# Base and levels of one-headed decay units issued and placed in three groups

## What is computed

```python
def chunked_vector_decay(q, k, v, log_f):        # o_t = S_t^T q_t, S_t = diag(exp(log_f_t)) S_{t-1} + k_t v_t^T
    def step(state, inp):
        qc, kc, vc, fc = inp
        cum = jnp.cumsum(fc, axis=-2)
        rel = jnp.where(causal, cum[..., :, None, :] - cum[..., None, :, :], -jnp.inf)
        scores = jnp.einsum('bhtd,bhsd,bhtsd->bhts', qc, kc, jnp.exp(rel))
        o = (jnp.einsum('bhts,bhsv->bhtv', scores, vc)
             + jnp.einsum('bhtd,bhdv->bhtv', qc * jnp.exp(cum), state))
        ...
```

## Time and profile before

| | |
|---|---|
| median of 3 executions | 3364.64 us |
| lowest, highest | 3363.71, 3365.63 us |
| the profiled execution | 3369.68 us |
| its span, first to last instruction | 3367.6 us |
| mean granted clock of TensorE, as a share of 2.4 GHz | 0.993 |

### The profile page before, as it was taken

One profiled execution on the slowest core, in us unless ns is written; L12 is line 12 of the kernel. 1 busy time (PEld: TensorE's weight loads), 2 busy tenths in 40 slices (PEclk: granted clock), 3 DMA queues, 4 the chain that ended last, 5 costly groups with the idle time before them and its releaser, 6 DMA issues. The chain is left out here.

```text
span 3367.6 us, 55457 instructions
## 1 busy us (share of the span) xinstructions
PE 3313.2 (98%) x23626; PEld 2746.0 (82%) x23626; DVE 2101.0 (62%) x2531; ACT 1602.6 (48%) x1893; POOL 313.2 (9%) x265
## 2 busy tenths in 40 slices
PE   9999999999999998999999999999999999999998
PEld 7887676778888887788888888888788888888887
DVE  7665453459988897756656663555676567753544
ACT  5332111338787875443356543533443356643432
POOL 0000000000111012000123110000000123120000
PEclk9999999999999999999999999999999999999999
DMA  6211442359999997122111111343122111111433
GB/s 230 78 56 54 168 162 76 140 217 396 415 415 415 414 414 297 70 76 88 52 64 52 45 64 51 106 182 125 67 71 83 58 46 58 40 62 51 157 124 112
DMA packets 97243, 492.92 MB, mean 146 GB/s; under 512 B 10920, under 2 KB 11432, under 8 KB 59104
## 3 DMA queue, kind: packets, MB, share of 16 engines
q1 hardware_dynamic: 77216, 417.31, 32.4%
q0 software_dynamic: 14160, 51.55, 4.4%
q10 hardware_dynamic: 5616, 20.45, 1.5%
HBM read 431.43 MB, written 57.84 MB: 145 GB/s over the span
## 5 line engine op out<-in xcount | busy, mean ns | idle before, releaser
L136 PE MATMUL ps<-HH,WS 128*128 128x512 f32 (+1 forms) x2576 | 1027.6, 399 | 4.7 <-DVE WS L1578 2.9
L138 PE MATMUL ps<-HH,WS 128*128 128x512 f32 (+1 forms) x2576 | 1006.2, 391 | 0.0
L137 PE MATMUL ps<-HL,WS 128*128 128x512 f32 (+1 forms) x1936 | 755.7, 390 | 0.0
L136 PEld LDWEIGHTS ps<-HH,WS 128*128 128x128 f32 (+1 forms) x2576 | 483.9, 188 | 112.4 <-DVE WS L1578 6.7
L138 PEld LDWEIGHTS ps<-HH,WS 128*128 128x128 f32 (+1 forms) x2576 | 483.4, 188 | 105.2
L1641 ACT ACTIVATE WA<-ps 128x512 f32<-128x512 f32 x240 | 142.7, 595 | 849.6 <-PE ps L138 814.1
L137 PEld LDWEIGHTS ps<-HL,WS 128*128 128x128 f32 (+1 forms) x1936 | 363.4, 188 | 73.9 <-issue 1.5
L136 PE MATMUL ps<-WAR 128*128 128x512 f32 x768 | 306.8, 399 | 0.9 <-DVE WAR L1372 0.9
L138 PE MATMUL ps<-WAR 128*128 128x512 f32 x768 | 301.1, 392 | 0.0
L1578 DVE TENSOR_TENSOR WS<-RAW,WS 128x1024 fp32r<-128x1024 f32 (+2 forms) x152 | 202.0, 1329 | 111.9 <-ACT WS L1573 111.9
L136 PE MATMUL ps<-WS,HH 128*128 128x256 f32 x896 | 259.4, 289 | 3.8 <-DVE WAR L2616 2.3
(11 more groups left out here) (418 smaller groups left out, 5309.8 us busy)
## 6 DMA issues: line engine op xcount, KB each, us to landing
WR<-in_weu SPq DMA_DIRECT2D x36, 1024.0 KB, 9.0
WR<-in_wed SPq DMA_DIRECT2D x36, 1024.0 KB, 8.6
WR<-in_weg SPq DMA_DIRECT2D x35, 1024.0 KB, 10.3
RAW<-in_wo SPq DMA_DIRECT2D x32, 1024.0 KB, 4.9
WA<-in_wada SPq DMA_DIRECT2D x48, 512.0 KB, 4.5
H<-in_weg SPq DMA_DIRECT2D x23, 1024.0 KB, 10.4
H<-in_weu SPq DMA_DIRECT2D x23, 1024.0 KB, 8.5
H<-in_wed SPq DMA_DIRECT2D x22, 1024.0 KB, 10.2
```

Source lines behind the costliest of these rows:

```text
L136: t.matmul(o, l[0], r[0], start=st, stop=False)
L137: t.matmul(o, l[0], r[1], start=False, stop=False)
L138: return t.matmul(o, l[1], r[0], start=False, stop=sp)
```

## The change

In one-headed units nothing is issued in core steps 0, 1, 3 and 5 for base and levels. Step 2 issues base, level 0 and level 1, step 4 levels 2 and 3, step 6 levels 4 and 5; level 6 stays in step 7. This holds for PE's products, for the banks and tiles in the plan, and for DVE's placements. The factors and exponentials stay in the steps where they were, and so does everything of two-headed units. No operation is added or taken away.

```diff
+        def together(U, l):
+            if count(U) > 1:
+                return (l,)
+            return (l - 1, l) if l % 2 else ()
 ...
@@ plan_decay
-                brief("base", U, n, end=("diag", U, n))
+                if count(U) > 1:
+                    brief("base", U, n, end=("diag", U, n))
             def products(l):
+                if l == 0 and count(U) == 1:
+                    brief("base", U, 0, end=("diag", U, 0))
 ...
                 yield
-                products(l)
+                for x in together(U, l):
+                    products(x)
@@ tensor_decay
+            def base():
                 for n in N:
                     free(t, banks, "base", U, n)
 ...
+            if count(U) > 1:
+                base()
             def products(l):
                 h = 1 << l
                 E = tl("E", U, l)
+                if l == 0 and count(U) == 1:
+                    base()
                 t.wait_ge(*at("fac", U, l))
 ...
             for l in range(6):
                 yield
-                products(l)
+                for x in together(U, l):
+                    products(x)
@@ vector_decay
-            for n in N:
+            def diagonal(n):
 ...
+            if count(U) > 1:
+                for n in N:
+                    diagonal(n)
             def products(l):
+                if l == 0 and count(U) == 1:
+                    diagonal(0)
 ...
                 yield
-                products(l)
+                for x in together(U, l):
+                    products(x)
```

More of the change, by code:

```diff
@@ L2005, in tensor_decay @@
             t.wait_ge(*at(*k_ready(U)))
-            for n in N:
-                free(t, banks, "base", U, n)
-            for c in range(8):
+            def base():
                 for n in N:
[L2010 to L2015, removed]
+                    free(t, banks, "base", U, n)
+                for c in range(8):
+                    for n in N:
+                        rows = head_rows(U, n)
+                        for b in range(0, 128, 32):
+                            o = t.matmul(ps("base", U, n)[b:b + 32, c * 32:(c + 1) * 32], c8(k)[rows, c, b:b + 32],
+                                         c8(q)[rows, c, b:b + 32], start=True, stop=True)
+                        if c == 7:
+                            o.then_inc(*up("scores", U, n, 0))
+            if count(U) > 1:
+                base()
             def products(l):
```

## The result

The changed kernel takes 3371.11 us (median of 11 runs, 3369.41 to 3376.9) against 3363.75 us for the kernel before in the same comparison (11 runs): ratio 1.0023, 95% interval 1.0016 to 1.0031. It is slower by 7.4 us where 6.2 us off were forecast. The time lies outside the range of 3356.4 to 3361.4, and on the side that had a chance of 0.04.

A forecast was written before the change was run, and what follows sets the result against it. PE, busy 98% of the span, was taken as the bound; 4.0 us from groups, 2.0 from unit 16 and 0.2 from unit 4 made 6.2 off 3364.64, giving 3358.4 us, range 3356.4 to 3361.4.

The forecast's parts named there:

- What bounds the kernel: Whole span: PE is busy for 98%, so only shortening PE's own sequence or its few waits moves the end.
- Groups put together: PE's small groups in the eight one-headed units: each joint saves about 0.24 us, 4.0 us in all.
- the cheap joint: Between joined groups on PE: the short pairs' joint, saving 0.27 us against groups alone; the dear one saves 0.17.
- The matmuls stay the same in number: One-headed units' base and levels: matmul counts unchanged; only how many groups stand alone changes.
- Units 7 and 19: Base there is hidden by the norm's waits, so moving it gains little: 0.1 us each, 0.2 together.
- Costs nothing there: Base between unit 6's outputs and its norm (units 7, 19): free today; without it the first wide matmul starts unchanged.
- Unit 16: Its PE waits hang on DVE; the scan comes 2.5 us earlier, giving 2.0 us beyond the groups' sum.
- about 0.5 us left: Unit 16, PE's wait before L1764: of 1.76 us about 0.5 stays after the change.
- What is late next: DVE's burst of 4.7 us in joined steps: still 1.3 us to spare in unit 16, so no harm.
- (c): Rival on PE's joined groups of three: joints cost as much as edges, groups gain 0; 3363.9 us, chance 0.08.
- (d): Rival in units 4 and 16: DVE's burst of copies becomes the bound, slower; 3382 or 3370 us, chance 0.04.
- starts inside the x192 group that gape by over 0.1 us: Sign in PE's timeline, joined group of base, levels 0 and 1: such gaps would show the inner joints wrong.

The follow-up runs named there:

- e2: Changed kernel with 80 more matmul records (160 instructions) put far ahead of the one-headed units, which stay as they are: 3370.43 us, ratio 1.0023.
- e3: Changed kernel regrouped in one-headed units: base with level 0, 1 with 2, 3 with 4, 5 with 6: 3360.5 us, ratio 0.999.
- e6: Changed kernel with longer groups: base and levels 0, 1, 2 at step 2, levels 3, 4, 5 at step 5: 3383.27 us, ratio 1.0058.
- e1: Changed kernel with base and its DVE mask back in step 0; levels 0+1, 2+3, 4+5 stay together: 3358.72 us, ratio 0.9984.
- e4: Changed kernel, but units 7 and 19 issue base at step 0 again; the other six keep the group of three: 3366.18 us, ratio 1.0008.
- e5: Pairs everywhere: units 7 and 19 cut as in e1, the other six one-headed units as in e3: 3358.74 us, ratio 0.9985.

## Why the prediction was wrong, step by step

**What bounds the kernel: right.** PE decides everywhere. That is also why a stall of PE goes into the time whole.

**Groups put together: the size right, the step incomplete.** Where no stall falls the forecast of the groups holds. Unit 17 was to gain 4 x 0.24 = 0.96 and gained 1.04. Unit 4 was to gain 0.48 + 0.2 and gained 0.87. The group of three, which was given 2.1 us, costs 1797.84 - 1795.33 - 0.45 = 2.06 in unit 4, counted as in the earlier trace rows from the last wide matmul to the second behind. These units even lie at the cheap joint, 1.04 / 4 = 0.26, near the 0.27 of the short pairs that every joint was to have by the rule of the Trainium skill (TensorEngine Tiling (Array Packing), Key Properties: a change of the tiling mode drains the engine, another tile of the same mode doesn't; it gives no figure). Here trace and rule agree.

The step that failed is the one under it: "The matmuls stay the same in number", and so costs beyond edges and joints weren't looked for. The rate at which instructions are used is a quantity of its own. The trace of before shows it: a lone x64 group uses 128 instructions in 0.67 us (1870.95 to 1871.62), a pair 256 in some 1.3, and wide matmuls with their weight loads 2 in 0.23. The forecast never put the 384 of the joined group beside the 256 of a block. The page's row for queue 8 had it: 16 KB a packet. Four of the eight groups, in units 5, 6, 16 and 19, then held a whole block, and PE stood still inside them; the three stalls that count and the clock behind them are 5.9 + 3 x 1.7 = 11 us, put at nothing in the sum. With the half-clock stretch behind unit 19's norm, 1.7, and unit 18's 0.7, that is some 13.4 lost, against 4.3 gained in the stretches: about the +8.7 of the table.

**Units 7 and 19: half right.** The base was to be free where it stood, hidden by the norm's waits. The changed kernel, start of unit 7:

```profile
1949.79 1.73 PE L1806 MATMUL ps<-WA 128*128 128x128 f32 x14
1951.95 0.47 PE L1842 MATMUL ps<-WAR,OR 128*128 128x512 f32 x1 [0.43 <-ACT WAR L1821]
1952.93 0.47 PE L1842 MATMUL ps<-WAR,OR 128*128 128x512 f32 x1 [0.51 <-ACT WAR L1821]
...
1954.50 0.50 PE L1845 MATMUL ps<-WAR,OR 128*128 128x512 f32 x1 [0.72 <-POOL WAR L1854]
1954.84 0.28 PE L136 MATMUL ps<-WS,HH 128*128 128x256 f32 x1
```

Against the earlier trace rows the waits before L1842 are longer and the wide matmul isn't earlier, and the stretch is 0.19 shorter: as forecast, 0.1, in kind and nearly in size. In unit 19 longer waits (0.71 for the second L1842, 0.68 for the last L1845) end in a half-clock stretch:

```profile
2949.71 0.76 PE L1845 MATMUL ps<-WAR,OR 128*128 128x512 f32 x1 [0.68 <-POOL WAR L1854]
2950.27 0.41 PE L136 MATMUL ps<-WS,HH 128*128 128x256 f32 x1
```

0.76 on record for L1845 in place of 0.50, and 0.41 for the wide one in place of 0.28. "Costs nothing there" left out the clock: PE stands idle for longer, and the next 3.4 us run at half speed. All four kernels with base out of this place of unit 19 have the stretch (the changed one at 2949.8, e2 at 2955.3, e3 at 2942.4, e6 at 2959.7), and the three with base in it (e1, e4, e5) don't. With base apart (e1) both units gain 0.7 to 0.8: base where it was and 0 joined with 1 is the better cut for them.

**Unit 16: the start right, the size wrong.** 2.0 us beyond the groups were forecast, with the scan 2.5 us earlier; the stretch shrank by 0.53. Unit 16 begins 2.24 us earlier in the changed kernel than in the one before (ACT's L1938 for level 2: 2787.13, and 2784.89), so 2.24 goes onto its times. DVE of the changed kernel:

```profile
2785.97 1.17 DVE L1947 TENSOR_TENSOR WA<-WA 128x512 f32<-128x512 f32 x1 [11.01 <-ACT WA L1938]
...
2788.51 2.10 DVE L1578 TENSOR_TENSOR WS<-RAW,WS 128x1024 fp32r<-128x1024 f32 x1
...
2796.17 1.22 DVE L2108 TENSOR_TENSOR WA<-ps,CT 128x1024 f32<-128x1024 f32 x1
...
2819.43 2.29 DVE L2283 TENSOR_TENSOR_SCAN WA<-RM,WA 128x1024 f32<-128x1024 f32 x1
```

The packed stretch starts at 2785.97 + 2.24 = 2788.21, where 2788.2 was forecast. The work up to the mask L2108 takes 10.2 us instead of 9.1, the scan comes at 2821.67 instead of 2819.7, only 0.53 before. The same operations are slower here than where I had read them: the weight split L1578 takes 2.10 us, and 1.22 at another place of the unit (2803.60). POOL works through its L1929 and L1930 until 2794.5 here; L1898 takes 1.58 us before that and 1.23 after it. That the two engines get in each other's way would fit, but no run tested it. 1.1 of the missing 2.0 us lies there; the rest is spread over the 23 us from the mask to the scan.

PE's stall is not the cause. In e2 unit 16 has no stall in its groups, only the one of 0.92 us behind the first, and DVE runs as in the changed kernel, 1.98 us later from end to end:

```profile
2787.95 1.17 DVE L1947 TENSOR_TENSOR WA<-WA 128x512 f32<-128x512 f32 x1 [11.01 <-ACT WA L1938]
...
2798.16 1.22 DVE L2108 TENSOR_TENSOR WA<-ps,CT 128x1024 f32<-128x1024 f32 x1
...
2821.41 2.29 DVE L2283 TENSOR_TENSOR_SCAN WA<-RM,WA 128x1024 f32<-128x1024 f32 x1
```

The stretch of unit 16 is 0.53 shorter in both. L1764 of e2, and of the changed kernel, in PE's timeline:

```profile
2827.36 1.80 PE L1764 MATMUL ps<-WA 128*128 128x128 f32 x14 [1.76 <-ACT WA L1748]
```

```profile
2825.37 0.80 PE L1764 MATMUL ps<-WA 128*128 128x128 f32 x5 [0.23 <-ACT WA L1748]
```

With the stall of 0.92 PE waits 1.76 us here, with that of 2.56 it waits 0.23: what the stall takes goes off the wait. The longest stall was free, because DVE sets this unit's end, as it does in unit 18. The forecast of "about 0.5 us left" met the observed 0.23 for a wrong reason.

**What is late next: looked at the wrong resource.** The burst on DVE does no harm at the requests for levels 2 to 5, where it was weighed, and the pattern of projections in steps is unchanged. It does harm at the unit's end, where it wasn't: 1.1 us at unit 18's L1764, since DVE there runs without idle time up to the scan. The feed of instructions wasn't on the list.

**The rivals.** (c) named the place: "A joined group of three doesn't run on as the pairs do". But it was priced by joints at 3363.9, with a gain of nothing, where a missing block costs some eight times the 0.24 of an edge. Its chance of 0.08 had nothing behind it, as the trace of before shows no group of three. (d) named the right engine for 1.1 us in one unit and the wrong place and size. The test that I named, starts inside the x192 group that gape by over 0.1 us, is the one that found it.

## What to carry over

Count the instructions of a burst, not only its time: here groups of 384 instructions, 1.9 us long, stalled in ten of 22 places by 1.7 to 2.7 us (the changed kernel, e2 and e4), and groups of up to 256 never did inside. Keep bursts of tiny matmuls at or under a block of 256 and put wide ones between them; then most of the same joins gain 5 us, where the longer ones lost 7. Work that fills a gap is best left there: base hidden behind the norm of units 7 and 19 cost nothing; moved, it cost unit 7 some 0.6 us (0.19 gained instead of 0.80) and unit 19 a stretch at half clock besides.

## What the runs showed of the hardware

**PE's program comes in blocks of 256 instructions (16 KB).** In the four kernels with groups of three or four all 22 stalls end at the same remainder of the instruction count, 163, and 1.2 to 1.5 us after the end of a packet of queue 8, which itself takes 0.9 to 1.8 us. From the entry of a block to the end of a stall of over 1.5 us behind it 3.1 to 4.2 us pass, of which a whole block of small matmuls fills some 1.2. In the runs with pairs, blocks that took 1.5 to 3 us had no stall behind them, and one of 1.20 us in e2 (unit 18) had none either; their packets had come earlier. How far ahead a packet is sent for varies, and what sets it stays open.

**A stall can halve the clock, but needn't.** Behind the stalls of units 5, 6 and 19 (1.83, 2.06 and 2.01 us) PE fell from 2.4 to 1.2 GHz; behind the longest, of 2.56 us in unit 16, and behind unit 4's of 2.59 us in e2, it didn't. What tells them apart wasn't found. In the changed kernel, e2, e3 and e6 the norm's waits at the start of unit 19, all under 1 us, were followed by such a stretch too; in e6 they were 0.43, 0.50 and 0.73, while in unit 7 of the changed kernel waits of 0.43, 0.51 and 0.72 weren't.
